# Expert rows weighted as they leave PSUM and added to the residual rows in DRAM by an indirect DMA, in place of a gather in the last stage

## The chip, the cores and the metric

The kernel runs on one core of a Trainium2 chip. The metric is the time of one execution on the device in microseconds (us); three runs of the kernel before took 2931.78, 2933.26 and 2941.8 us, so its median is 2933.26 us. Lower is better.

## What is computed

One layer of a decoder trunk on 2048 tokens of 1024 features, all in float32: RMSNorm, differential attention with a residual add, RMSNorm, a mixture of 32 SwiGLU experts, and a last RMSNorm. The change touches the mixture and what follows it:

```python
g_p   = max(softmax(h @ w_group + b_group))              # 4 groups of 8 experts
top_v, top_i = top_k(e_logits[chosen group], 2)          # two experts per token
top_w = softmax(top_v) * g_p                             # the routing weight
...
# rows sorted by expert, each expert padded to whole blocks of 128 rows
yr = (silu(xb @ w_gate[e]) * (xb @ w_up[e])) @ w_down[e]  # block by block
y  = zeros((T, D)).at[row_tok].add(yr * row_w[:, None])
x  = x + y
out = rms_norm(x, norm_final)
```

So each token gets two expert rows, each times its weight, added to its residual row.

## The kernel before, in words

The program is five stages, each with its own instruction stream per engine, hand-placed semaphores and a barrier between stages: `project` (QKV), `attend`, `mix_and_route`, `run_experts`, `finish`.

**attend** also writes zeros to the spare blocks of the expert output buffer `y_rows`: 32 DMAs of 512 KB from `nil` (L469), spread over the loads of `q_st`.

**mix_and_route** takes the 16 tiles of 128 tokens through a software pipeline five steps deep. Step n on TensorE (PE) is: output projection of tile n-1 (L1164), transpose of tile n (L1172), transpose of tile n-2 (L1179), router matmul of tile n-3 (L1187), rank counts of tile n-4 (L1194). ScalarE (ACT) squares and roots, copies `oT_hi` out of PSUM (L984), and last in its step copies `h2T` (L989). VectorE (DVE) forms x2 and h2, picks experts for tile n-4 (`choose`), places tile n-5 (`place`), and then, as the last thing of its step, writes `oT_lo` of tile n (L1062); the next projection waits for that and for the next x2 (L1039). GpSimd (POOL) scatters each token number into the list `slots` in DRAM (L953). The logits are kept in SBUF (`kept`) for the last stage.

**run_experts** loops over n = 45 blocks of 128 rows (32 experts, each at least one block, read from a table in SBUF). The two splits of every weight, hi on ACT and lo on DVE, make the matmuls three-term. The order of the work is the program order of each engine:

```python
# PE, iteration b
gate_up(b)        # 48 matmuls of 512 columns
turn_x(b + 1)     # waits for the gathered rows of block b+1
down(b)           # 24 matmuls; `down(k)` is of block k-1
turn_h(b)
# POOL, iteration b: waits for turn_x(b-1), loads 128 list entries
# (L1288), waits for them, gathers 128 rows of h2 into xg (L1290)
```

ACT, iteration b: a quarter of the next expert's `gu_hi` split, `act_g`, `x_high(b+1)`, the other three quarters, `take_y(b)` (PSUM to `y_sb`, L1321), `d_hi`, `hT_hi`, then `store_y(b)`: a plain store of 512 KB into `y_rows` (L1325). `take_y` waits for the store before it (semaphore `y_out`). SyncE (SP) loads the 6 MB of weights of the next expert as the splits free the raw buffers (L1270, L782, L783). There are one `xg`, one `listed` and one `y_sb`.

**finish** computes the 16 x 2 routing weights at once, then goes through the tiles in a ring of four: SP loads x2, POOL gathers the two expert rows of each token (L1571, two DMAs of 512 KB a tile), DVE does two multiply-adds (L1627, L1630), ACT square and root, DVE scales, SP stores.

## Time and profile before

| | before |
|---|---|
| median of three runs (lowest, highest) | 2933.26 us (2931.78, 2941.8) |
| profiled execution, span from first to last instruction | 2934.6 us |
| PE / DVE / ACT / POOL busy | 82% / 57% / 43% / 19% |
| `project` | up to about 600 us |
| `attend` | up to about 1564 us |
| `mix_and_route` | up to about 1913 us |
| `run_experts` | up to about 2832 us |
| `finish` | to the end, 103 us |

No own time of the profiled execution stands beside its span in what is shown; the span is 1.3 us above the median of the runs and inside their spread. The stages follow one another with a barrier between them, so each stage's own limit counts in full. The busy shares over the whole span say little, since each stage has another limit: a stage has to be read by its own windows, waits and timeline.

### The profile page before, as it was taken

The numbers are of one execution on the slowest core, as the hardware profiler recorded it, in microseconds if no ns is written. First come the engines' busy times: TensorE is split into PE (matmuls) and PEld (weight loads), VectorE is DVE, ScalarE is ACT, GpSimd is POOL, SyncE is SP. The second block draws the span as 40 slices with busy tenths as digits, with TensorE's granted clock in tenths as the row PEclk, the third lists the DMA queues.
The fourth block names the chain that finished last, engine by engine and source line by source line (L and its number), as shares of the span: only waits on it lengthen the run. The fifth ranks groups of instructions, "written<-read, shape, count | busy, mean of one in ns | idle before, by whom it ended". The sixth has DMA issues, their size and how long they took to land. (4 is left out here: it accounts for less than half of the span.)

```text
span 2934.6 us, 44327 instructions
## 1 busy us (share of the span) xinstructions
PE 2406.7 (82%) x12888; PEld 2029.3 (69%) x12888; DVE 1679.4 (57%) x3485; ACT 1272.2 (43%) x2083; POOL 558.9 (19%) x432
## 2 busy tenths in 40 slices
PE   5999999937687887877885999667899999999930
PEld 4888889926576676766774788555788888787730
DVE  6122122127687776876895566555665665665656
ACT  5111111115475665655774222145554555555533
POOL 0000000004353343443441011110010110111123
PEclk7999999969898998998997999778999999999965
DMA  4333333264515425244122443157768667768758
GB/s 165 115 122 114 122 127 107 90 172 119 147 28 135 108 72 141 68 109 133 59 71 95 176 132 115 51 221 280 297 254 299 251 238 283 291 255 304 277 223 329
DMA packets 263134, 491.03 MB, mean 167 GB/s; under 512 B 24425, under 2 KB 125969, under 8 KB 258898
## 3 DMA queue, kind: packets, MB, share of 16 engines
q1 hardware_dynamic: 218306, 397.31, 39.4%
q0 software_dynamic: 17072, 53.79, 5.6%
q10 hardware_dynamic: 27616, 38.28, 3.9%
q8 instruction: 60, 0.98, 0.1%
q14 instruction: 80, 0.66, 0.1%
HBM read 363.71 MB, written 125.60 MB: 167 GB/s over the span
## 5 line engine op out<-in xcount | busy, mean ns | idle before, releaser
L1372 DVE TENSOR_TENSOR gu_lo<-gu_raw,gu_hi 128x2048 fp32r<-128x2048 f32 x128 | 293.2, 2291 | 162.2 <-ACT gu_hi L1303 118.0
L728 PE MATMUL ps_s<-k_lo,q_st 128*128 128x512 f32 (+3 forms) x640 | 275.7, 431 | 133.7 <-DMA q_st<-qk 68.6
L523 ACT ACTIVATE prob<-prob,shift 128x1024 f32<-128x1024 f32 (+7 forms) x384 | 342.8, 893 | 4.2
L752 PE MATMUL ps_o<-v_hl,aT_hi 128*128 128x256 f32 x1088 | 294.4, 344 | 59.9 <-DVE aT_lo L685 59.0
L608 DVE TENSOR_SCALAR_CACHE_REDUCE prob<-ps_s 128x128 f32<-128x128 f32 (+7 forms) x352 | 276.9, 787 | 114.4 <-PE ps_s L728 111.2
L1303 ACT ACTIVATE gu_hi<-gu_raw 128x2048 fp32r<-128x2048 f32 x128 | 239.0, 1908 | 178.8 <-DMA gu_raw<-in_moe_w_up 101.4
L207 DVE TENSOR_TENSOR stage<-ps,stage 128x512 fp32r<-128x512 f32 (+1 forms) x128 | 71.3, 557 | 427.1 <-ACT stage L162 427.1
L550 ACT ACTIVATE aT_hi<-ps_t 128x512 fp32r<-128x512 f32 (+2 forms) x320 | 168.2, 526 | 306.2 <-PE ps_t L740 223.8
L752 PEld LDWEIGHTS ps_o<-v_hl,aT_hi 128*128 128x128 f32 x1088 | 208.7, 192 | 91.8 <-DVE aT_lo L685 86.8
L162 ACT ACTIVATE stage<-ps 128x512 fp32r<-128x512 f32 (+1 forms) x128 | 62.8, 491 | 474.4 <-PE ps L258 314.8
L508 POOL TENSOR_TENSOR prob<-prob 128x384 f32<-128x384 f32 (+6 forms) x112 | 254.5, 2272 | 9.3
L728 PEld LDWEIGHTS ps_s<-k_lo,q_st 128*128 128x128 f32 x640 | 131.0, 205 | 167.1 <-issue 74.1
L728 PE MATMUL ps_s<-k_hi,q_st 128*128 128x512 f32 (+3 forms) x640 | 245.5, 390 | 0.0
L754 PE MATMUL ps_o<-v_hl,aT_lo 128*128 128x128 f32 x1088 | 244.4, 225 | 0.0
L1464 PE MATMUL ps_g<-gu_hi,xT_lo 128*128 128x512 f32 x720 | 236.6, 410 | 4.3 <-DVE xT_lo L1387 3.6
L1464 PE MATMUL ps_g<-gu_lo,xT_hi 128*128 128x512 f32 x720 | 231.3, 403 | 0.0
L685 DVE TENSOR_TENSOR aT_lo<-ps_t,aT_hi 128x512 fp32r<-128x512 f32 (+2 forms) x320 | 193.1, 605 | 64.8 <-ACT aT_hi L550 64.1
L1464 PE MATMUL ps_g<-gu_hi,xT_hi 128*128 128x512 f32 x720 | 230.0, 400 | 0.0
L506 POOL TENSOR_SCALAR prob<-prob,coef 128x384 f32<-128x384 f32 (+6 forms) x112 | 116.9, 1044 | 581.7 <-DVE coef L646 581.7
L754 PEld LDWEIGHTS ps_o<-v_hl,aT_lo 128*128 128x128 f32 x1088 | 211.7, 195 | 3.6
L1380 DVE TENSOR_TENSOR d_lo<-d_raw,d_hi 128x2048 fp32r<-128x2048 f32 x64 | 146.8, 2294 | 95.7 <-ACT d_hi L1310 81.4
L740 PE MATMUL ps_t<-ident,prob 128*128 128x128 f32 x1088 | 180.7, 283 | 14.5 <-POOL prob L508 9.1
(227 smaller groups left out, 4673.6 us busy)
## 6 DMA issues: line engine op xcount, KB each, us to landing
gu_raw<-in_moe_w_gate SPq DMA_DIRECT2D x128, 512.0 KB, 7.7
gu_raw<-in_moe_w_up SPq DMA_DIRECT2D x128, 512.0 KB, 8.6
d_raw<-in_moe_w_down SPq DMA_DIRECT2D x64, 1024.0 KB, 4.9
qk<-stage SPq DMA_DIRECT2D x64, 512.0 KB, 2.7
y_rows<-y_sb ACTq DMA_DIRECT2D x45, 512.0 KB, 3.4
v<-stage SPq DMA_DIRECT2D x64, 256.0 KB, 2.1
q_st<-qk SPq DMA_DIRECT2D x256, 64.0 KB, 2.4
y_rows<-nil SPq DMA_DIRECT2D x32, 512.0 KB, 3.4
```

Of the source, the lines that this page charges most:

```text
L508: pool.tensor_tensor(p0, p0, p1, ALU.add).then_inc(mixed_p, 1)
L523: nc.scalar.activation(prob[:, r % RING, m, k0:k0 + w], prob[:, r % RING, m, k0:k0 + w], ACT.Exp, bias=shift[:, r % 4, m:m + 1], scale=SCA ...
L550: nc.scalar.activation(aT_hi[:, g % 4, 0:n], ps_t[:, g % 2, 0:n], ACT.Copy).then_inc(t_hi, 1)
L608: ins = nc.vector.tensor_scalar(prob[:, r % RING, m, k0:k0 + far], ps_s[:, c % 2, 0:far], 1.0, None, ALU.mult, ALU.max, accum_out=top[:, r ...
L685: nc.vector.tensor_tensor(aT_lo[:, g % 4, 0:w], ps_t[:, g % 2, 0:w], aT_hi[:, g % 4, 0:w].bitcast(F32), ALU.subtract).then_inc(t_lo, 1)
L728: mm = pe.matmul(ps_s[:, c % 2, j:j + n], q_st[:, x % Q_RING, m, :], k_op[:, half % 2, m, k0 + j:k0 + j + n], start=k_op is k_lo, stop=k_o ...
L740: mm = pe.transpose(ps_t[:, g % 2, (k - k0) * P:(k - k0 + 1) * P], prob[:, r % RING, 0, k * P:(k + 1) * P], ident[:, :])
L752: pe.matmul(ps_o[:, x % 2, 0:2 * P], aT_hi[:, g % 4, t], v_hl[:, half, k, :], start=k == 0, stop=False)
L754: mm = pe.matmul(ps_o[:, x % 2, 0:P], aT_lo[:, g % 4, t], v_hl[:, half, k, 0:P], start=False, stop=k == i)
L1303: nc.scalar.activation(gu_hi[:, j * GC:(j + 1) * GC], gu_raw[:, j], ACT.Copy).then_inc(gu_hi_set, 1)
L1372: nc.vector.tensor_tensor(gu_lo[:, j * GC:(j + 1) * GC], gu_raw[:, j], gu_hi[:, j * GC:(j + 1) * GC].bitcast(F32), ALU.subtract).then_inc( ...
L1464: mm = pe.matmul(ps_g[:, half, :], x[:, cs], w[:, c, half, :], start=c == 0 and k == 0, stop=c == KC - 1 and k == 2)
```

## The change

The routing weights are computed in `mix_and_route`, tile by tile: DVE writes the five exponents' arguments to `x5` in `choose`, ACT does the Exp at the end of its step, DVE waits for that in `place` and writes token number and weight side by side into `tokw`; the scatter to `slots` moves eight bytes a row. In `run_experts` ACT multiplies by the weight as it takes the block from PSUM, ACT's store is gone, and POOL adds the 128 rows into `x2_rows` in DRAM by an indirect DMA with `compute_op=add`. POOL waits for each add to land, then loads the list again into `to_rows` for the next block. Padding rows point to 128 spare rows at the end of `x2_rows` and `h2_rows`. The 32 DMAs of zeros in `attend` become two. `finish` keeps all 16 tiles in SBUF, loads them without a ring and has no gather and no multiply-add. Line numbers in the two `order` blocks marked "of the change" are those of the changed kernel.

```diff
-            spare = scratch["y"].rearrange("(b p) d -> b p d", p=P)[EXPERTS:]
-            PER_PAIR = (BLOCKS_MAX - EXPERTS) // PAIRS
-            EVERY = (NR - Q_RING) // PER_PAIR
+            for rows_ in (scratch["h2"], scratch["x2"]):
+                sp.dma_start(rows_[SEQ:SEQ + P].rearrange("p (k d) -> p k d", k=4),
+                             nil[:, :].unsqueeze(1).to_broadcast([P, 4, D // 4])).then_inc(nil_out, 16)
             def pair(it, more):
...
-                    if (r - Q_RING) % EVERY == 0 and n < PER_PAIR:
-                        sp.dma_start(spare[bass.ds(it * PER_PAIR + n, 1)]
-                                     .rearrange("o p (k d) -> (o p) k d", k=4),
-                                     nil[:, :].unsqueeze(1).to_broadcast([P, 4, D // 4])).then_inc(nil_out, 16)
...
                     for k in range(2):
                         pool.indirect_dma_start(scratch["slots"], bass.IndirectOffsetOnAxis(ap=slot[:, q, k:k + 1], axis=0),
-                                                tok[:, q:q + 1], None).then_inc(scattered, 16)
+                                                tokw[:, q, k, :], None).then_inc(scattered, 16)
...
+                if has(at, 5):
+                    q = 1 - par
+                    act.wait_ge(chosen, (n - 5) * 13 + 13)
+                    nc.scalar.activation(e5[:, q, :], x5[:, q, :], ACT.Exp).then_inc(exped, 1)
...
+            nc.vector.tensor_scalar(empty[:, :, 0], lanes[:, :], P - 1, SEQ, ALU.bitwise_and, ALU.bitwise_or
+                                    ).then_inc(empty_set, 1)
...
+                nc.vector.tensor_scalar(x5[:, q, 0:GROUPS_E], lg[:, 0:GROUPS_E], gm[:, 0:1], None, ALU.subtract)
...
+                nc.vector.tensor_tensor(x5[:, q, 4:5], ev[:, 1:2], ev[:, 0:1], ALU.subtract)
...
+                gate(dve, exped, t + 1, passed)
+                link(nc.vector.tensor_reduce(e_sum[:, :], e5[:, q, 0:GROUPS_E], AX.X, ALU.add))
+                link(nc.vector.scalar_tensor_tensor(out=den[:, :], in0=e5[:, q, 4:5], scalar=1.0, in1=e_sum[:, :],
+                                                    op0=ALU.add, op1=ALU.mult))
+
                 dve.wait_ge(freed, t + (FREED0 - 1))
-                link(nc.vector.tensor_copy(tok[:, q:q + 1], tok_f[:, 0:1]))
+                weight = tokw[:, q, :, 1].bitcast(F32)
+                link(nc.vector.reciprocal(weight[:, 0:1], den[:, :]))
+                link(nc.vector.tensor_tensor(weight[:, 1:2], weight[:, 0:1], e5[:, q, 4:5], ALU.mult))
+                nc.vector.tensor_copy(tokw[:, q, :, 0], tok_f[:, 0:1].to_broadcast([P, 2]))
                 link(nc.vector.tensor_tensor(before[:, :], before[:, :], both[:, q, :], ALU.add))
...
-            pool.iota(iota_i[:, :], pattern=[[1, EXPERTS]], base=0, channel_multiplier=0).then_inc(iota_set, 1)
             n = blocks_of(pool)
-            with pool.Fori(0, n + 1) as b:
...
+            def load_x(b):
...
                 gate(pool, x_turned, b + X_TURNED0, passed)
...
                 gate(pool, listed_in, b * 16 + 16, passed)
                 pool.indirect_dma_start(xg[:, :], None, scratch["h2"],
                                         bass.IndirectOffsetOnAxis(ap=listed[:, 0:1], axis=0)).then_inc(x_in, 16)
+
+            def load_rows(k):
+                at = look(pool, k - 1, COL_LIST, 0, SLOTS - P)
+                pool.dma_start(to_rows[:, :], scratch["slots"][bass.ds(at, P), :]).then_inc(rows_in, 16)
+
+            def add_y(k):
+                gate(pool, y_taken, k + Y_TAKEN0, passed)
+                pool.indirect_dma_start(scratch["x2"], bass.IndirectOffsetOnAxis(ap=to_rows[:, 0:1], axis=0),
+                                        y_sb[:, :], None, compute_op=ALU.add).then_inc(y_out, 16)
+
+            load_x(0)
+            load_x(1)
+            load_rows(1)
+            with pool.Fori(1, n) as b:
+                load_x(b + 1)
+                add_y(b)
+
+                gate(pool, y_out, b * 16, passed)
+                load_rows(b + 1)
+            add_y(n)
+            pool.wait_ge(y_out, n * 16)
+            pool.sem_inc(passed, 1)
...
                 act.wait_ge(d_used, k * DS + D_USED0)
-                act.wait_ge(y_out, k * 16 + (Y_OUT0 - 16))
-                nc.scalar.activation(y_sb[:, :], ps_y[:, :], ACT.Copy).then_inc(y_taken, 1)
-
-            def store_y(k):
-                gate(act, y_taken, k + Y_TAKEN0, passed)
-                act.dma_start(scratch["y"].rearrange("(b p) d -> b p d", p=P)[bass.ds(k - 1, 1)].rearrange("o p d -> (o p) d"),
-                              y_sb[:, :]).then_inc(y_out, 16)
+                act.wait_ge(rows_in, k * 16)
+                nc.scalar.activation(y_sb[:, :], ps_y[:, :], ACT.Copy, scale=to_rows[:, 1:2].bitcast(F32)).then_inc(y_taken, 1)
...
                 nc.scalar.activation(hT_hi[:, :], ps_h[:, :], ACT.Copy).then_inc(h_hi_set, 1)
-                if not first:
-                    store_y(b)
...
+        GROUPS = (0, 1, 2, 2, 3, 3, 3, 3, 4, 4, 4, 4, 5, 5, 5, 5)
+        x_in = [s(f"x_in{k}") for k in range(6)]
...
+            for t in range(TILES):
+                sp.dma_start(acc[:, t, :], x2_rows[t]).then_inc(x_in[GROUPS[t]], 16)
+                if t == 0:
+                    sp.dma_start(g_row[:, :], io["norm_final"].rearrange("(o d) -> o d", o=1).to_broadcast([P, D])).then_inc(g_in, 16)
+            for t in range(TILES):
                 gate(sp, done, t + 1, passed)
-                sp.dma_start(out_rows[bass.ds(t, 1)].rearrange("o p d -> (o p) d"), acc[:, i, :]).then_inc(stored[i], 16)
...
-                    for k in range(2):
-                        pool.indirect_dma_start(y[:, i, k, :], None, scratch["y"],
-                                                bass.IndirectOffsetOnAxis(ap=rows[:, i, k:k + 1], axis=0)).then_inc(y_in[i], 16)
...
+            for t in range(TILES):
+                act.wait_ge(x_in[GROUPS[t]], 16 * GROUPS.count(GROUPS[t]))
+                if t:
+                    act.wait_ge(squared, t)
+                nc.scalar.activation(sq[:, :], acc[:, t, :], ACT.Square, accum_out=ss[:, t:t + 1]).then_inc(squared, 1)
+                act.wait_ge(squared, t + 1)
+                nc.scalar.activation(rt[:, t:t + 1], ss[:, t:t + 1], ACT.Sqrt, bias=eps[:, 0:1], scale=1.0 / D).then_inc(rooted, 1)
...
+            for t in range(TILES):
+                dve.wait_ge(rooted, t + 1)
+                nc.vector.reciprocal(ri[:, t:t + 1], rt[:, t:t + 1]).then_inc(inverted, 1)
+                dve.wait_ge(inverted, t + 1)
+                nc.vector.scalar_tensor_tensor(out=acc[:, t, :], in0=acc[:, t, :], scalar=ri[:, t:t + 1], in1=g_row[:, :],
                                                op0=ALU.mult, op1=ALU.mult).then_inc(done, 1)
...
-            with dve.Fori(0, TILES // RING) as q:
-                for i in range(RING):
-                    dve.wait_ge(x_in[i], q * 16 + 16)
-                    dve.wait_ge(y_in[i], q * 32 + 32)
-                    a = acc[:, i, :]
-                    nc.vector.scalar_tensor_tensor(out=a, in0=y[:, i, 0, :], scalar=w_all[:, 0, bass.ds(q * RING + i, 1)],
-                                                   in1=a, op0=ALU.mult, op1=ALU.add).then_inc(mixed, 1)
-                    dve.wait_ge(mixed, q * RING + (i + 1))
-                    nc.vector.scalar_tensor_tensor(out=a, in0=y[:, i, 1, :], scalar=w_all[:, 1, bass.ds(q * RING + i, 1)],
-                                                   in1=a, op0=ALU.mult, op1=ALU.add).then_inc(added, 1)
...
-            "slots": nc.dram_tensor("slots", (SLOTS, 1), I32).ap(),
-            "y": nc.dram_tensor("y_rows", (BLOCKS_MAX * P, D), F32).ap(),
+            "x2": nc.dram_tensor("x2_rows", (SEQ + P, D), F32).ap(),
+            "h2": nc.dram_tensor("h2_rows", (SEQ + P, D), F32).ap(),
+            "slots": nc.dram_tensor("slots", (SLOTS, 2), I32).ap(),
```

GpSimd in the loop of `run_experts`, of before: one list load and one gather an iteration (`ISA` and `REGISTER_ALU` are waits and register work, `TENSOR_LOAD` reads the block table).

```order
L1256 TENSOR_LOAD block_table
L1256 ISA x2
L36 REGISTER_ALU
L1288 REGISTER_ALU
L1288 DMA listed<-slots 128x1
L36 ISA
L1290 DMA xg<-h_rows,listed 128x1024
L1284 ISA
L1284 COMPARE_AND_BRANCH
```

The same loop of the change, from the list load of `load_x(b + 1)` to the loop's end:

```order
L1289 DMA listed<-slots 128x2
L29 ISA
L1291 DMA xg<-h_rows,listed 128x1024
L1300 DMA x_rows<-y_sb,to_rows 2176x1024
L29 REGISTER_ALU
L1257 ISA
L1257 TENSOR_LOAD block_table
L1257 ISA x2
L1296 ISA
L1296 DMA to_rows<-slots 128x2
L1306 REGISTER_ALU
L1306 COMPARE_AND_BRANCH
```

The add stands behind the gather of the next block, and the next iteration's list load and gather stand behind the add, its landing and the load of `to_rows`.

ScalarE in one step of the loop of `mix_and_route`, of before:

```order
L972 ACTIVATE sq,ss<-x 128x1024
L974 ACTIVATE rt<-ss,eps 128x1
L976 ISA
L978 ACTIVATE sq<-o_t 128x1024
L980 ACTIVATE rth<-ssh,eps 128x8
L981 REGISTER_ALU
L984 ACTIVATE oT_hi<-ps_a,sub_gs 128x1024
L989 ACTIVATE h2T<-ps_c 128x1024
```

The same step of the change:

```order
L966 ACTIVATE sq,ss<-x 128x1024
L968 ACT_TABLE_LOAD
L968 ACTIVATE rt<-ss,eps 128x1
L970 ISA
L972 ACTIVATE sq<-o_t 128x1024
L974 ACTIVATE rth<-ssh,eps 128x8
L975 REGISTER_ALU
L978 ACTIVATE oT_hi<-ps_a,sub_gs 128x1024
L983 ACTIVATE h2T<-ps_c 128x1024
L986 ISA
L987 ACT_TABLE_LOAD
L987 ACTIVATE e<-x 128x5
```

The Exp stands last in the step, with a table load of its own, and the root of the next step needs a second one.

## Rows read from the trace of the kernel before

**Rows 1.** Windows: us, PE, PEld, DVE, ACT, POOL; clock, DMA share, GB/s
```profile
1930.00:2828.00 898.00, 838.72 (x3786) 677.03 (x3784) 546.28 (x329) 476.33 (x367) 94.80 (x90) 0.96 0.72 266
2832.00:2935.00 103.00, 0.00 (x0) 0.00 (x0) 64.03 (x71) 34.90 (x59) 45.59 (x49) 0.50 0.88 331
```

**Rows 2.** Timeline of TensorE, second and last turn of gathered rows: start us, us
```profile
1947.60 1.04 PE L1453 MATMUL ps_x<-ident,xg 128*128 128x128 f32 x8
...
2805.12 1.03 PE L1453 MATMUL ps_x<-ident,xg 128*128 128x128 f32 x8
```

**Rows 3.** Timeline of a block with weights to split and one without
```profile
2308.96 1.03 PE L1453 MATMUL ps_x<-ident,xg 128*128 128x128 f32 x8
...
2316.36 1.01 ACT L1321 ACTIVATE y_sb<-ps_y 128x1024 f32<-128x1024 f32 x1
...
2327.05 1.04 PE L1453 MATMUL ps_x<-ident,xg 128*128 128x128 f32 x8
...
2333.79 1.03 ACT L1321 ACTIVATE y_sb<-ps_y 128x1024 f32<-128x1024 f32 x1 [4.65 <-PE ps_y L1486]
```

**Rows 4.** Waits, 1920 to 2830 us: us in total, times, longest
```profile
POOL listed L1288 <- PE ps_x L1453: 574.2, 45, 20.2
```

**Rows 5.** Timeline of GpSimd in the stretch of rows 3
```profile
2310.72 0.57 POOL L1288 DMA_DIRECT2D listed<-slots  x1 [12.76 <-PE ps_x L1453]
2313.79 2.25 POOL L1290 DMA_INDIRECT xg<-h_rows,listed  x1 [2.50 <-DMA listed<-slots]
2328.82 0.57 POOL L1288 DMA_DIRECT2D listed<-slots  x1 [12.78 <-PE ps_x L1453]
2335.42 0.97 POOL L1290 DMA_INDIRECT xg<-h_rows,listed  x1 [6.03 <-DMA listed<-slots]
```

**Rows 6.** Landing of two gathers (L1290), issued at 2241.4 and 2335.4 us
```profile
DMA to landing us min/median/max: 4.2/4.2/4.2
...
DMA to landing us min/median/max: 7.9/7.9/7.9
```

**Rows 7.** DMA issues of the whole run: KB each, median us to landing
```profile
y_rows<-y_sb ACTq DMA_DIRECT2D x45, 512.0 KB, 3.4
...
xg<-h_rows,listed POOLq DMA_INDIRECT x46, 6.9
```

**Rows 8.** GpSimd: first table look (ns, first start us) and first list load
```profile
L1256 POOLq TENSOR_LOAD <-block_table x47: 289/296/697, 1914.8 to 2765.8; - x47
...
1917.23 0.61 POOL L1288 DMA_DIRECT2D listed<-slots  x1 [3.64 <-issue]
```

**Rows 9.** Timeline of SyncE: the first load of the next weights
```profile
2326.49 0.37 SPq L782 DMA_DIRECT2D gu_raw<-in_moe_w_gate  x1
```

**Rows 10.** Timeline of TensorE after an idle stretch
```profile
2820.69 1.22 PE L1486 MATMUL ps_y<-d_hi,hT_lo 128*128 128x512 f32 x2 [8.50 <-DVE hT_lo L1411]
...
2824.48 0.63 PE L1486 MATMUL ps_y<-d_hi,hT_hi 128*128 128x512 f32 x2
```

**Rows 11.** Timeline of one tile of the routing stage
```profile
1680.16 1.28 DVE L1062 SCALAR_TENSOR_TENSOR oT_lo<-ps_a,sub_gs,oT_hi 128x1024 fp32r<-128x1024 f32 x1 [0.79 <-ACT oT_hi L984]
...
1681.66 1.02 ACT L989 ACTIVATE h2T<-ps_c 128x1024 f32<-128x1024 f32 x1 [1.53 <-PE ps_d L1187]
...
1682.72 5.50 PE L1164 MATMUL ps_b<-wo_hi,oT_lo 128*128 128x512 f32 x16 [0.72 <-DVE x L1039]
```

**Rows 12.** Timeline: a table load and an Exp on ScalarE in the last stage
```profile
2832.36 1.28 ACT L1578 ACT_TABLE_LOAD   x1 [3.31 <-PEq L1210]
...
2833.81 0.20 ACT L1579 ACTIVATE e_v<-e_v 128x16 f32<-128x16 f32 x1
```

**Rows 13.** Waits, 600 to 1700 us
```profile
PE ps_s L728 <- DMA q_st<-qk: 68.6, 6, 13.1
```

**Rows 14.** Timeline of GpSimd where the weights come late: two successive list loads
```profile
2008.76 0.57 POOL L1288 DMA_DIRECT2D listed<-slots  x1 [18.44 <-PE ps_x L1453]
...
2036.38 0.57 POOL L1288 DMA_DIRECT2D listed<-slots  x1 [19.46 <-PE ps_x L1453]
```

More of the change, by code:

```diff
@@ L843, in mix_and_route @@
         ps_e = ctx.enter_context(nc.psum_tensor("ps_e", [P, 512], F32))
-        ident, start, kept, e_all, rank_all = (keep[k] for k in ("ident", "start", "kept", "e_all", "rank_all"))
+        ident, start = keep["ident"], sb("start", [P, EXPERTS])
         s = lambda name: sem("c_" + name)
@@ L931, in _ @@
         def _(pool):
-            pool.memset(zeros[:, :], 0).then_inc(made, 1)
+            pool.memset(empty[:, :, :], 0).then_inc(made, 1)
             pool.memset(ones[:, :], 1.0).then_inc(made, 1)
@@ L963, in _ @@
             act.wait_ge(gain_set, 1)
-            act.wait_ge(made, 9)
+            act.wait_ge(made, 10)
             def step(n, par, at):
@@ L1066, in choose @@
             def choose(t, q):
-                link = chain(chosen, t * 14)
+                link = chain(chosen, t * 13)
                 dve.wait_ge(routed, t + (1 + ROUTED0))
@@ L1152, in _ @@
             pe.sem_inc(h2T_set, H2T0)
-            pe.wait_ge(made, 10)
+            pe.wait_ge(made, 11)
             def step(n, par, at):
@@ L1235, in run_experts @@
         ps_y = ctx.enter_context(nc.psum_tensor("ps_y", [P, D], F32))
-        ident, start, e_all, rank_all, dest = (keep[k] for k in ("ident", "start", "e_all", "rank_all", "dest"))
+        ident = keep["ident"]
         s = lambda name: sem("d_" + name)
@@ L1519, in finish @@
-        w_all = sb("w_all", [P, 2, TILES])
         eps = sb("eps55", [P, 1])
-        ss, rt, ri = sb("ss5", [P, RING]), sb("rt5", [P, RING]), sb("ri5", [P, RING])
-        kept, dest = keep["kept"], keep["dest"]
+        ss, rt, ri = sb("ss5", [P, TILES]), sb("rt5", [P, TILES]), sb("ri5", [P, TILES])
         s = lambda name: sem("e_" + name)
-        g_in, x_in, y_in = s("g_in"), [s(f"x_in{i}") for i in range(RING)], [s(f"y_in{i}") for i in range(RING)]
-        rows_set, weigh, exped, mixed, eps_set = s("rows"), s("weigh"), s("exped"), s("mixed"), s("eps")
@@ L1543, in _ @@
-            for i in range(RING):
-                load(i, i)
-            def store(t, i):
-                gate(sp, done, t + 1, passed)
-                sp.dma_start(out_rows[bass.ds(t, 1)].rearrange("o p d -> (o p) d"), acc[:, i, :]).then_inc(stored[i], 16)
-            with sp.Fori(0, TILES // RING - 1) as q:
-                for i in range(RING):
-                    store(q * RING + i, i)
-                    if i >= 1:
-                        load(q * RING + (RING + i - 1), i - 1)
-                load(q * RING + (2 * RING - 1), RING - 1)
@@ L1556, in _ @@
-            for i in range(RING):
-                store(TILES - RING + i, i)
-            for i in range(RING):
-                sp.wait_ge(stored[i], 16 * TILES // RING + STORED0)
+            for t in range(TILES):
[3 more added lines that the diff above has]
+            for t in range(TILES):
+                gate(sp, done, t + 1, passed)
+                sp.dma_start(out_rows[t], acc[:, t, :]).then_inc(stored, 16)
@@ L1563, in _ @@
             pool.memset(eps[:, :], 1e-6).then_inc(eps_set, 1)
-            with pool.Fori(0, TILES // RING) as q:
-                for i in range(RING):
-                    gate(pool, added, q * RING + (i + 1), passed)
-                    pool.tensor_copy(rows[:, i, :], dest[:, bass.ds(q * (2 * RING) + 2 * i, 2)]).then_inc(rows_set, 1)
-                    gate(pool, rows_set, q * RING + (i + 1), passed)
-                    for k in range(2):
-                        pool.indirect_dma_start(y[:, i, k, :], None, scratch["y"],
-                                                bass.IndirectOffsetOnAxis(ap=rows[:, i, k:k + 1], axis=0)).then_inc(y_in[i], 16)
```

123 lines of the change are left out of this document (22 added, 101 removed).

## The prediction

> **What bounds the kernel now.** The stages are separated by barriers, so I read each by itself. The windows come first: in the expert stage TensorE is busy 839 of 898 us at a granted clock of 0.96, the DMA engines 72% [rows 1]. That stage is bound by TensorE. The last stage is bound by its DMAs: 103 us at a DMA share of 0.88 and 331 GB/s, with no engine above 64 us [rows 1]. The timeline then gives the length of a block. From the second turn of gathered rows to the last, 44 blocks later, pass 2805.12 - 1947.60 = 857.5 us, 19.5 a block [rows 2]; two blocks at full speed are 2327.05 - 2308.96 = 18.1 us apart [rows 3]. The waits say why GpSimd never held TensorE up: it waits 574 us in 45 waits, 12.8 us each, for the turn that frees `xg` [rows 4]. Its list load and gather run ahead of the need, during one whole block.
>
> **The experts: a chain closes.** This part decides. TensorE's order is `gate_up(b)`, `turn_x(b+1)`, `down(b)`. In the change GpSimd's list load and gather for `turn_x(b+2)` stand behind `add_y(b)`, behind the wait for its landing and behind the load of `to_rows`. `add_y(b)` waits for `take_y(b)`, that for `down(b)`, and that stands on TensorE behind `turn_x(b+1)`. So from one turn to the next runs one chain, and nothing in it overlaps; only `gate_up` lies beside it. Its parts:
>
> 1. Turn to the end of `take_y`: with weights to split 2316.36 + 1.01 - 2308.96 = 8.4 us, without 2333.79 + 1.03 - 2327.05 = 7.8 us [rows 3]. ACT's multiply by a weight in place of a plain copy is costed at nothing: it is the same instruction with another scale. The store that leaves ACT's queue stood behind other work: nothing.
> 2. Semaphore to GpSimd's DMA: the turn ends at 2309.99, the list load starts at 2310.72: 0.7 us [rows 3, 5].
> 3. The add to its landing: no row has an adding DMA. The nearest is the indirect gather of the same 128 rows of 4 KB, median 6.9 us; the plain store of the same tile lands in 3.4 us, and gather and store one after the other are 7.9 + 3.4 = 11.3 us [rows 6, 7]. I take 6.9: same queue, same rows, DRAM read as well. The ends are 3.4 and 11.3; it can't be less than nothing, since GpSimd waits for it.
> 4. From landing to the next list load: a look into the table, the load of `to_rows`, another look. The first two looks and one issue took 1917.23 - 1914.8 = 2.4 us [rows 8]; with 0.57 for the second DMA and 0.6 before it, 3.6 us.
> 5. List load to gather: 2313.79 - 2310.72 = 3.1 us where no weights were just issued, 2335.42 - 2328.82 = 6.6 us behind them [rows 5].
> 6. Gather to landing: 4.2 us alone, 7.9 us behind weights [rows 6].
>
> The weights of the next expert are issued once DVE has split the last ones, 2326.49 - 2308.96 = 17.5 us behind the turn [rows 3, 9]; the list load comes 8.4 + 0.7 + 6.9 + 3.6 = 19.6 us behind it, right after them. So where there are weights the dear values hold: 8.4 + 0.7 + 6.9 + 3.6 + 6.6 + 7.9 = 34.1 us. Where there are none: 7.8 + 0.7 + 6.9 + 3.6 + 3.1 + 4.2 = 26.3 us. `gate_up` of the next block starts behind `down` and ends before the gather has landed. Of 44 periods 31 have weights (32 experts, one loaded ahead): 31 x 34.1 + 13 x 26.3 = 1399 us, against 857.5: **+542 us**. TensorE will idle some 16 of 34 us. After 8.5 idle us a pair of matmuls took 1.22 us where 0.63 is usual [rows 10], which lasts some 3 us, so 1.5 us are lost; with weights this hides behind ACT's splits, which end as late as `down`, without it lengthens the chain: 13 x 1.5 = **+20 us**.
>
> A page of the Trainium skill prices the transfers lower: "DMA: Bandwidth & Descriptors", in its section on the anatomy of a DMA on the gpsimd path, gives about 2.0 us plus bytes over 436 GB/s, which is an estimate of 3.2 us for 512 KB and 2.0 for the list. By that the period would be 8.4 + 0.7 + 3.2 + 3.6 + 2.0 + 3.2 = 21.1 us, and the stage only +71 us. The trace does not agree: a gather alone needs 4.2 us and one behind weights 7.9 [rows 6].
>
> **The routing stage.** Today `oT_lo` starts at 1680.16 and the projection that waits for it and for x2 at 1682.72 [rows 11]; VectorE has a little slack before it. In the change `place` stands in front of `oT_lo` and waits for the Exp, which ACT does at the end of its step, behind `h2T`: 1681.66 + 1.02 = 1682.68 [rows 11], then a table load of 1.28 and the Exp, 0.2 [rows 12]: 1684.2. Then six small operations, costed at the 0.2 of the Exp beside them: `oT_lo` starts at 1685.4, 5.2 us later, and TensorE has nothing left to do. Steps 5 to 15 pay it in full, 57 us; of the five steps that drain the pipeline the first pays 5.2 and the others some 1.2 each for the longer `place`: 10 us. Colder restarts of TensorE, as above: 8. Together **+75 us**, between 40 (if half hides) and 107 (6.7 us in all 16 steps). The second table load, before the root, lies beside the projection. The larger list to clear and the wider scatter stand on GpSimd, which first scatters over 100 us into the stage: nothing; without that cover they would cost a microsecond or two.
>
> **The last stage.** It moved 103 us x 331 GB/s = 34 MB. Without the 32 gathers 17.3 MB are left; at the same rate 52 us. **-51 us.** ACT's squares and roots lie beside: with them ACT was busy only 34.9 of 103 us [rows 1]. If latency at both ends tells more, -40; at the best rate, -58.
>
> **The rest.** In the attention stage 30 stores of zeros go. TensorE waits 68.6 us for `q_st` in six waits [rows 13]; a store of 512 KB ahead of it can cost about a microsecond each: **-5 us**, at most -68. The last add lands later than the last store did: **+4 us**.
>
> **Sum.** 2934.6 + 542 + 20 + 75 - 51 - 5 + 4 = 3520 us. This is made against the span of the profiled execution, 1.3 us above the median of the runs, which changes nothing here.
>
> **Rivals.**
> - *Hidden anyway (faster).* The add, its list and their waits cost GpSimd 6.9 + 3.6 + 0.7 = 11.2 us a block, and it idles 12.8 [rows 4]; so the expert stage stays at 19.5 a block, the last stage saves 51, and the Exp is hidden too: 2934.6 - 51 - 5 + 10 = 2889 us. It decides if the chain is shorter than 19.5 us. Against it: the idle time of GpSimd lies before the turn, and the add can't start before `down`. 3 in 100, and 1 in 100 that it comes out level.
> - *Bare transfers.* The DMA load falls with the longer period, and all transfers cost their quiet price: 8.4 + 0.7 + 3.4 + 3.6 + 3.1 + 4.2 = 23.4 us with weights, 22.8 without: 1022 us, +164, in all about 3140. 4 in 100. The rule of the page above points this way.
> - *The weights bind instead.* As before, but where weights come late the blocks were already 2036.38 - 2008.76 = 27.6 us apart [rows 14], since loads, splits and `take_y` make a loop of their own. 31 x 27.6 + 13 x 22.8 = 1152 us, +295: about 3270. 12 in 100.
> - *A dear add.* It reads its destination as well as its source, and takes 11.3 us: + 4.4 x 44 = 194, about 3715. 10 in 100. "Collectives: The Full Stack" of the Trainium skill, on why ReduceScatter is half of AllGather, says that an add emits two reads for one write; no row here shows it.
>
> **How the numbers follow.** 70 in 100 for the forecast, whose own range is 3400 to 3650. The range of 3250 to 3680 takes in the third rival and the near part of the fourth and leaves out the rest. A measurement can tell about 0.5% here, 15 us. Faster 0.03, within 0.01, slower 0.96: only the first rival is not slower.
>
> **What would show it.** In the changed profile turns of gathered rows (the PE rows of `ps_x`) stand some 34 and 26 us apart; TensorE waits there for the DMA of `xg`, over 450 us in total; GpSimd waits for `y_sb` and for the add's landing. The adding DMA lands in about 7 us. In the routing stage VectorE waits for ACT's Exp and a tile takes some 5 us more than before. The last stage takes some 52 us. I am wrong if TensorE still turns rows every 20 us, or if the list load overtakes the add.

## The result, and the profile after

The change makes the kernel slower by a fifth: median 3525.35 us (3522.68 to 3527.32, four runs) against 2934.98 us (2931.78 to 2941.8, four runs), a ratio of 1.2004 with a 95% interval of 1.1986 to 1.2021. The profiled execution took 3522.68 us, its span is 3520.5 us. The prediction was 3520, with a range of 3250 to 3680.

The windows of the changed kernel, from the second turn of gathered rows to the last, from there to the last stage, and the last stage (us; busy us of PE, PEld, DVE, ACT, POOL; granted clock, DMA share, GB/s):

```profile
2030.50:3435.10 1404.60, 883.92 (x3673) 711.44 (x3671) 534.61 (x316) 470.84 (x359) 205.70 (x174) 0.82 0.52 166
3435.10:3475.00 39.90, 16.08 (x60) 12.70 (x60) 6.50 (x4) 7.34 (x6) 3.85 (x3) 0.71 0.17 26
3475.00:3520.00 45.00, 0.00 (x0) 0.00 (x0) 22.09 (x32) 23.07 (x49) 0.10 (x1) 0.50 0.97 385
```

They answer to [rows 1]. The 44 periods that took 857.5 us now take 1404.6. No engine and no queue is full in them: TensorE is busy 63% of the time, where it was over 90%, and the DMA share fell to 0.52. Of the stages, the last alone became shorter. The waits between 1930 and 3500 us (us in total, times, longest) show who waits for whom:

```profile
POOL x_rows L1300 <- ACT y_sb L1344: 681.5, 45, 17.7
...
PE ps_x L1443 <- DMA xg<-h_rows,listed: 543.8, 44, 24.9
...
POOL to_rows L1296 <- issue: 313.9, 44, 10.8
...
POOL xg L1291 <- DMA listed<-slots: 184.6, 45, 6.3
```

TensorE, which never waited for `xg`, waits 543.8 us for it in 44 waits. GpSimd's wait moved from the turn [rows 4] to `y_sb`, and 313.9 us stand in front of the load of `to_rows`, put down to "issue"; that is the wait for the add to land, which the code puts there and the profile doesn't name. One whole period in the timeline (TensorE, ScalarE, GpSimd; start us, us):

```profile
2595.98 1.97 PE L1443 MATMUL ps_x<-ident,xg 128*128 128x128 f32 x8 [12.42 <-DMA xg<-h_rows,listed]
...
2604.31 1.10 ACT L1344 ACTIVATE y_sb<-ps_y,to_rows 128x1024 f32<-128x1024 f32 x1
...
2606.30 3.38 POOL L1300 DMA_INDIRECT x_rows<-y_sb,to_rows  x1 [13.65 <-ACT y_sb L1344]
2615.79 0.59 POOL L1296 DMA_DIRECT2D to_rows<-slots  x1 [6.10 <-issue]
2617.46 0.55 POOL L1289 DMA_DIRECT2D listed<-slots  x1 [1.08 <-issue]
2623.85 1.02 POOL L1291 DMA_INDIRECT xg<-h_rows,listed  x1 [5.84 <-DMA listed<-slots]
...
2630.99 1.97 PE L1443 MATMUL ps_x<-ident,xg 128*128 128x128 f32 x8 [15.30 <-DMA xg<-h_rows,listed]
```

This is the chain of the prediction, link by link: 9.4 us from the turn to the end of `take_y`, 0.9 to the add, 9.5 until it has landed and `to_rows` is asked for, 1.7 to the list load, 6.4 to the gather, 7.1 to the turn: 35.0 us.

In the routing stage VectorE and ScalarE do this in front of one projection:

```profile
1757.26 1.02 ACT L983 ACTIVATE h2T<-ps_c 128x1024 f32<-128x1024 f32 x1 [1.53 <-PE ps_d L1192]
1758.30 1.28 ACT L987 ACT_TABLE_LOAD   x1
1759.60 0.21 ACT L987 ACTIVATE e<-x 128x5 f32<-128x5 f32 x1
...
1759.93 0.16 DVE L1104 TENSOR_REDUCE e_sum<-e 128x1 f32<-128x4 f32 x1 [7.89 <-ACT e L987]
...
1761.09 1.28 DVE L1062 SCALAR_TENSOR_TENSOR oT_lo<-ps_a,sub_gs,oT_hi 128x1024 fp32r<-128x1024 f32 x1
1762.28 1.21 DVE L1039 TENSOR_TENSOR x<-ps_b,x 128x1024 f32<-128x1024 f32 x1
```

VectorE idles 7.89 us for the Exp. `oT_lo` starts 3.8 us behind the start of `h2T`; in [rows 11] it started 1.5 us before it. That is 5.3 us later.

Where the 585.9 us between the two spans went:

| part | forecast | measured | from |
|---|---|---|---|
| start and attention | -5 | +4.8 | first projection of the routing stage 1597.0, now 1601.8 |
| routing | +75 | +78.1 | second turn 1947.6, now 2030.5, less 4.8 |
| 44 periods | +542 + 20 | +547.1 | 857.5, now 1404.6 |
| last turn to the last stage | +4 | +12.9 | 2805.1 to 2832.3, now 3435.1 to 3475.2 |
| last stage | -51 | -57.0 | 102.3, now 45.3 |

### The profile page after: what moved, and what is told of

Same layout as the page of the kernel before. It is cut to its first block and busy times, and to the rows that moved or that the text cites. A ratio compares the mean times of both kernels' runs of the same rounds, so it can differ in the third digit from the quotient of the medians.

```text
span 3520.5 us, 44205 instructions
## 1 busy us (share of the span) xinstructions
PE 2502.9 (71%) x12888; PEld 2103.1 (60%) x12888; DVE 1642.6 (47%) x3473; ACT 1309.5 (37%) x2120; POOL 631.3 (18%) x474
## 5 line engine op out<-in xcount | busy, mean ns | idle before, releaser
L1443 PE MATMUL ps_x<-ident,xg 128*128 128x128 f32 x368 | 88.7, 421 | 543.8 <-DMA xg<-h_rows,listed 543.8
L1443 PEld LDWEIGHTS ps_x<-ident,xg 128*128 128x128 f32 x368 | 70.9, 220 | 563.0 <-DMA xg<-h_rows,listed 562.7
L716 PE MATMUL ps_s<-k_lo,q_st 128*128 128x512 f32 (+3 forms) x640 | 274.3, 429 | 138.5 <-DMA q_st<-qk 74.2
L1399 DVE TENSOR_TENSOR xT_lo<-ps_x,xT_hi 128x1024 fp32r<-128x1024 f32 x46 | 56.3, 1224 | 492.3 <-ACT xT_hi L1337 492.3
L1337 ACT ACTIVATE xT_hi<-ps_x 128x1024 fp32r<-128x1024 f32 x46 | 47.2, 1027 | 515.2 <-PE ps_x L1443 515.2
L1300 POOL DMA_INDIRECT x_rows<-y_sb,to_rows x45 | 112.8, 2507 | 681.5 <-ACT y_sb L1344 681.5
## 6 DMA issues: line engine op xcount, KB each, us to landing
k_lo<-qk SPq DMA_DIRECT2D x28, 512.0 KB, 13.3
```

Of the source, the lines that this page charges most:

```text
L716: mm = pe.matmul(ps_s[:, c % 2, j:j + n], q_st[:, x % Q_RING, m, :], k_op[:, half % 2, m, k0 + j:k0 + j + n], start=k_op is k_lo, stop=k_o ...
L1300: pool.indirect_dma_start(scratch["x2"], bass.IndirectOffsetOnAxis(ap=to_rows[:, 0:1], axis=0), y_sb[:, :], None, compute_op=ALU.add).then ...
L1443: mm = pe.transpose(ps_x[:, c * P:(c + 1) * P], xg[:, c * P:(c + 1) * P], ident[:, :])
```

## The experiments

The chain was the theory. Its rivals after the result: the adding DMA is dear wherever it stands; the loop of the weights (their loads and splits) binds; the Exp costs by its operations, not by its place. Landings are counted from the start of the issue. Each run's times are the medians, each ratio is against the kernel before on the same chip.

**1. The gather ahead of the add**

```diff
             load_rows(1)
+            load_x(2)
             with pool.Fori(1, n) as b:
-                load_x(b + 1)
+                load_x(b + 2)
                 add_y(b)
...
             add_y(n)
+            pool.wait_ge(x_in, n * 16 + 32)
```

> Only GpSimd's order changes: list load and gather of block b+2 stand ahead of the add of block b-1, and no longer behind it, its landing and the load of to_rows. Everything else of the changed kernel, the adds too, stays. Theory (the chain from turn to turn closes through the add): a turn frees xg, list load and gather run beside down and gate_up as in the kernel before, the turns come back to about 19.7 us apart, 44 x 19.7 = 867 us in place of the 1406 us measured from the second turn to the last, so about 3525 - 539 = 2986 us (2960 to 3010), and TensorE's wait for xg is under 60 us. Rival (the adding DMA itself is too dear: it takes 1.6 to 3.4 us of GpSimd, lands in 7.8 and holds up the transfers beside it): turns stay over 27 us apart and the time over 3300.

Measured: 3010.68 us, ratio 1.0249 (1.0225 to 1.0272): 515 us came back by moving one call. The periods sum to 897.7 us. The chain is the cause of nearly all of the loss, and the dear-add rival falls. TensorE's wait for `xg` fell to 42.2 us. But the time is 0.7 us above the range that I gave: 40 us are missing in the periods, 20.4 us each and not 19.5. GpSimd's timeline in this kernel says where a part of them is:

```profile
2436.47 1.01 POOL L1291 DMA_INDIRECT xg<-h_rows,listed  x1 [5.36 <-DMA listed<-slots]
2437.78 3.37 POOL L1300 DMA_INDIRECT x_rows<-y_sb,to_rows  x1 [0.30 <-issue]
2449.90 0.59 POOL L1296 DMA_DIRECT2D to_rows<-slots  x1 [8.75 <-issue]
2451.58 0.55 POOL L1289 DMA_DIRECT2D listed<-slots  x1 [1.09 <-issue]
2454.68 1.02 POOL L1291 DMA_INDIRECT xg<-h_rows,listed  x1 [2.55 <-DMA listed<-slots]
```

GpSimd waits for nobody there but its own DMAs: gather to gather are 18.2 us, with 12.1 from the start of the add to the load of `to_rows`, which waits for its landing. It has become as long as a block. Without the list's wait 20 us of the missing time come back (experiment 6 against 5), and experiment 10 finds the rest.

**2. The add without the sum**

```diff
-                                        y_sb[:, :], None, compute_op=ALU.add).then_inc(y_out, 16)
+                                        y_sb[:, :], None).then_inc(y_out, 16)
```

> The indirect DMA writes its rows without adding; the sum with the residual and of the two experts is left out. Same chain, same rows and bytes to write. Theory (the chain counts the landing in full, and reading the destination is part of the 7.8 us): the landing falls to about 5, GpSimd's issue to 1.0, so 44 x 3 = 130 us off, about 3395 (3330 to 3450). Rival (the add as such is free, 7.8 us is what any scatter of 128 rows takes here): within 15 us of 3525. Second rival (only the issue is dearer): 44 x 1.5 = 66 off, and the landing counted from the issue's end stays.

Measured: 3438.45 us, ratio 1.1697 (1.1678 to 1.1717), 87 us off; the periods sum to 1323.0 us, 1.9 us less each. The landings of this line, in the changed kernel and here (here up to 3380 us, without the last one):

```profile
DMA to landing us min/median/max: 6.1/7.8/12.6
```

```profile
DMA to landing us min/median/max: 3.4/4.7/9.8
```

The median landing falls by 3.1 us, and 1.9 of it reach the period. The rest meets the same traffic one link on: the gather behind it lands in 5.9 us (median) and no longer in 4.4. The theory holds in kind; its 3 us a period were too many. The first rival (the add as such is free) falls. So does the second (only the issue is dearer): the issue falls from 2.5 to 1.8 us on average, and the landing counted from its end still falls from 5.7 to 3.6. The packets of GpSimd's queue (packets, MB, share of the 16 engines' span), in the changed kernel and here:

```profile
q0 software_dynamic: 20448, 60.96, 7.5%
```

```profile
q0 software_dynamic: 20448, 60.96, 5.1%
```

Same packets and same bytes. With the sum they keep the DMA engines 0.075 x 3520.5 - 0.051 x 3437.1 = 89 us longer, 2.0 us an add. What an add costs the DMA engines can't be read from the bytes in these traces.

**3. The list ahead, the gather behind the add**

```diff
+            def load_list(b):
                 at = look(pool, b, COL_LIST, 0, SLOTS - P)
+                gate(pool, x_in, b * 16, passed)
+                pool.dma_start(listed[:, :], scratch["slots"][bass.ds(at, P), :]).then_inc(listed_in, 16)
...
             with pool.Fori(1, n) as b:
                 load_x(b + 1)
+                load_list(b + 2)
                 add_y(b)
```

> The list for the next gather is loaded as soon as the gather before has landed, ahead of the add; the gather itself stays behind the add. Theory (chain terms add up one by one): the list's 6.4 us behind weights and 3.1 us without leave the chain, 31 x 6.4 + 13 x 3.1 = 239 us off, about 3286 (3240 to 3330). Rival (the list only waits out a burst of weight traffic that the gather would then meet): the gather's landing grows by what the list saves, and less than 120 us come off. Second rival (the loop of the weights binds at 27.6 us): the periods with weights stop at 27.6 and TensorE's waits turn from xg to the weights' splits.

Measured: 3361.11 us, ratio 1.1437 (1.1417 to 1.1456), 164 us off: between the theory's 239 and the rival's 120. The periods are 3.7 us shorter. The list's landing left the chain, and the gather's landing grew from a median of 4.4 us to 7.2 (line of the gather, in the changed kernel and here):

```profile
DMA to landing us min/median/max: 4.1/4.4/7.9
```

```profile
DMA to landing us min/median/max: 4.2/7.2/7.9
```

So these links of the chain do not simply add up: one of them waits out traffic that the next would meet. TensorE still waits for `xg` 380.8 us, so the loop of the weights doesn't bind even at 28 us a period.

**4. The Exp at the head of ScalarE's step**

```diff
             def step(n, par, at):
+                if has(at, 5):
+                    q = 1 - par
+                    act.wait_ge(chosen, (n - 5) * 13 + 13)
+                    nc.scalar.activation(e5[:, q, :], x5[:, q, :], ACT.Exp).then_inc(exped, 1)
                 if has(at, 2):
...
                     nc.scalar.activation(h2T[:, :], ps_c[:, :], ACT.Copy).then_inc(h2T_set, 1)
-                if has(at, 5):
-                    q = 1 - par
-                    act.wait_ge(chosen, (n - 5) * 13 + 13)
-                    nc.scalar.activation(e5[:, q, :], x5[:, q, :], ACT.Exp).then_inc(exped, 1)
```

> Only the routing stage changes: ACT does the Exp of tile n-5 at the head of its step, ahead of Square and Sqrt, and not behind the copy of h2T. Theory (VectorE waits for that Exp just before it writes oT_lo, on which the next projection hangs): the wait goes, the tile period falls from 23.7 us towards 17.3 plus at most 1.3 for a table load ahead of the root, so 16 tiles x 4 to 6 = 64 to 96 us off, of the 78 us that the stage grew by; about 3455 (3435 to 3475). Rival (the added small operations on VectorE and the two table loads a step are the cost, wherever the Exp stands): less than 25 us off.

Measured: 3449.29 us, ratio 1.1734 (1.1714 to 1.1753), 76 us off. In the trace the second turn moves from 2030.5 to 1960.0, 70.6 us, and the periods stay at 1404.3 in sum. Three successive tiles start their projections so:

```profile
1689.44 3.88 PE L1169 MATMUL ps_b<-wo_hi,oT_lo 128*128 128x512 f32 x16 [1.07 <-DVE x L1039]
1706.59 6.76 PE L1169 MATMUL ps_b<-wo_hi,oT_lo 128*128 128x512 f32 x16 [1.62 <-DVE x L1039]
1725.26 3.88 PE L1169 MATMUL ps_b<-wo_hi,oT_lo 128*128 128x512 f32 x16 [0.72 <-DVE x L1039]
```

They are 17.9 us apart on average. Two in the changed kernel are 23.7 us apart:

```profile
1739.82 6.61 PE L1169 MATMUL ps_b<-wo_hi,oT_lo 128*128 128x512 f32 x16 [1.35 <-DVE x L1039]
...
1763.55 2.93 PE L1169 MATMUL ps_b<-wo_hi,oT_lo 128*128 128x512 f32 x6 [1.19 <-DVE x L1039]
```

The place was the cost. Both table loads and the small operations are still there and cost some 8 us in the whole stage.

**5. Both orders together**

The edits of experiments 1 and 4, of which the two calls that move:

```diff
-                load_x(b + 1)
+                load_x(b + 2)
                 add_y(b)
...
             def step(n, par, at):
+                if has(at, 5):
+                    q = 1 - par
+                    act.wait_ge(chosen, (n - 5) * 13 + 13)
+                    nc.scalar.activation(e5[:, q, :], x5[:, q, :], ACT.Exp).then_inc(exped, 1)
```

> The edits of e1_gather_first and e4_exp_first together. Theory (two separate causes, which add up): the turns of e1 (897.7 us from the second to the last) and the routing stage of e4 (70.6 us shorter than in the changed kernel), so 3010.7 - 70.6 = about 2940 us (2930 to 2950), level with the kernel before. Rival (the two share a cover): over 2960.

Measured: 2942.55 us, ratio 1.0022 (1.0012 to 1.0031), within the theory's range. The two causes are separate and add up.

**6. The lists ahead as well**

```diff
             with pool.Fori(1, n) as b:
-                load_x(b + 1)
+                load_x(b + 2)
                 add_y(b)
+                load_list(b + 3)
```

> As e5_first_and_first, and each list is loaded as soon as the gather before it has landed, beside the landing of the add. Theory (in e1 GpSimd's own row of waits, list 4 + gather 1.3 + add 3 + landing 6 to 10 + next loads 1.7 us, had become as long as a block, and made it 20.4 us in place of 19.5): without the list's wait it has 4 us to spare, the turns take the 857.5 us of the kernel before or up to 8 more, and the time is 2940 - 35 = about 2905 us (2890 to 2920), faster than before. Rival (the adds' traffic holds up the weights): the turns stay above 885 us and the time above 2925.

Measured: 2923.16 us, ratio 0.9955 (0.9942 to 0.9969): the one version with the full sum that is faster than both kernels, 12 us faster than the kernel before. It is 3 us above the range that I gave. GpSimd has slack again (it waits 305.6 us for `y_sb`), and 36 of the 44 periods are 18.1 us, as in the kernel before. The periods sum to 881.7 us, though, 24 more than before. They lie in the seven long ones: 28.9 to 32.3 us, where the kernel before had 25.5 to 29.6. So the theory holds for the short periods, and something like the rival for the long ones; experiment 10 tests that.

**7. The zeros put back**

```diff
+                    n = (r - Q_RING) // EVERY
+                    if (r - Q_RING) % EVERY == 0 and n < PER_PAIR:
+                        sp.dma_start(spare[bass.ds(it * PER_PAIR + n, 1)]
+                                     .rearrange("o p (k d) -> (o p) k d", k=4),
+                                     nil[:, :].unsqueeze(1).to_broadcast([P, 4, D // 4])).then_inc(nil_out, 16)
```

> The changed kernel with the 32 stores of zeros of the attention stage put back, into rows that nothing reads. In the trace of before the first projection of the routing stage starts at 1597.0, in those of the changed kernel and four versions of it at 1599.4 to 1601.8, and TensorE waits 74 to 76 us for q_st in place of 68.6. Theory (the stores cost nothing, and by spacing the loads of q_st they even helped by 3 us): q_st back to 67 to 71 us, first projection near 1597. Rival (those microseconds lie in something else): q_st stays at 74 to 76. Second rival (my term of -5): q_st over 78.

Measured: 3520.51 us, ratio 1.1984 (1.1966 to 1.2003), whose interval overlaps that of the changed kernel. First projection at 1602.9, wait for `q_st`:

```profile
PE ps_s L725 <- DMA q_st<-qk: 72.8, 6, 13.4
```

None of the three theories, as far as one trace tells: with the stores back the wait is 72.8 us, without them 74.2 in the changed kernel, with the kernel before at 68.6. The stores of zeros cost and bring nothing that shows.

**8. Thin splits on VectorE**

```diff
-                    nc.vector.tensor_tensor(gu_lo[:, j * GC:(j + 1) * GC], gu_raw[:, j],
-                                            gu_hi[:, j * GC:(j + 1) * GC].bitcast(F32), ALU.subtract).then_inc(gu_split, 1)
+                    nc.vector.tensor_tensor(gu_lo[:, j * GC:(j + 1) * GC, :, 0:16], gu_raw[:, j, :, :, 0:16],
+                                            gu_hi[:, j * GC:(j + 1) * GC, :, 0:16].bitcast(F32), ALU.subtract).then_inc(gu_split, 1)
```

and the same for `d_lo`; both are set to zero once ahead of the loop.

> The changed kernel with VectorE's splits of the weights cut to 16 columns of each row; the low parts of the weights are left out otherwise. In the trace of the changed kernel GpSimd's issue of the add takes 1.64 us in 14 of 45, and up to 3.4 in the others, longer by as much as a 128x2048 split of VectorE runs beside it. Theory (GpSimd can't write the descriptors while VectorE runs such an operation): all 45 issues take 1.6 to 1.7 us, and about 40 us come off the chain for it, more if the weights land earlier; the landing behind the issue stays at 5.9 to 10. Rival (the DMA traffic stretches the issue): the issues still spread from 1.6 to 3.4.

Measured: 3503.25 us in one run. The line of the add (instructions, ns min/median/max), first in the changed kernel between 2020 and 3270 us, then here:

```profile
L1300 POOL DMA_INDIRECT x_rows<-y_sb,to_rows x38: 1639/2458/3420, 2054.9 to 3250.1; - x38
```

```profile
L1300 POOL DMA_INDIRECT x_rows<-y_sb,to_rows x43: 1635/1647/1679, 2051.0 to 3399.6; - x43
...
DMA to landing us min/median/max: 7.5/8.0/9.4
```

On the issue the theory's numbers are right: all 45 take 1.62 to 1.68 us. Its reason is another matter (last section). On the time it isn't right: the periods sum to 1392.4 us, 12 less and not 40. From the start of the add to the load of `to_rows` it is 9.67 us on average, against 9.70. What the issue saves, the landing takes: in the changed kernel (between 2050 and 2700 us) it had been

```profile
DMA to landing us min/median/max: 6.1/7.9/11.7
```

so its minimum rose from 6.1 to 7.5 us. The splits free the raw buffers earlier here: behind the add at 2477.0 us the next load of `d_raw` is issued after 1.4 us and the add lands in 7.9, behind the one at 2482.7 us of the changed kernel it is issued after 3.5 us and the add lands in 6.3. So more weights may be under way; that part wasn't tested.

**9. List and gather between the add's issue and its landing**

```diff
             load_rows(1)
+            load_x(2)
             with pool.Fori(1, n) as b:
-                load_x(b + 1)
                 add_y(b)
+                load_x(b + 2)
```

> The changed kernel, but GpSimd puts list load and gather between the issue of the add and the wait for its landing: they stand behind add and down still, no longer behind landing and to_rows. Theory (the wait on the landing and the to_rows load are terms of the chain, GpSimd's queue of DMAs is none): 7.8 + 1.7 us leave each period, so 32 - 9 = 23 us a turn and about 3525 - 400 = 3125 us (3060 to 3200). Rival (the DMAs of GpSimd's queue run one after the other, so list and gather wait for the add's bytes anyway): only to_rows' 1.7 us and little more goes, 3400 or above.

Measured: 3297.77 us, ratio 1.1236 (1.1217 to 1.1255): 225 us off, between both. The periods sum to 1180.6 us, 5.1 less each. GpSimd's timeline:

```profile
2441.37 3.36 POOL L1300 DMA_INDIRECT x_rows<-y_sb,to_rows  x1 [13.35 <-ACT y_sb L1346]
2444.14 1.21 POOL L1289 DMA_DIRECT2D listed<-slots  x1
2453.93 1.00 POOL L1291 DMA_INDIRECT xg<-h_rows,listed  x1 [8.58 <-DMA listed<-slots]
2455.14 0.57 POOL L1296 DMA_DIRECT2D to_rows<-slots  x1 [0.22 <-issue]
```

The list, 1 KB, needs 9.8 us to the gather behind an add, and as soon as the gather is issued the add has landed too (0.22 us of waiting). This is so all through the stage: in 42 of 44 blocks the list lands 0.1 to 0.4 us behind the add, in two 1.6 and 1.9 us. So a small load behind the add in the same queue came home with it, not before. Add with its landing, `to_rows` and list were 9.7 + 1.7 + 4.6 = 16 us of each period in the changed kernel (means over all periods); from the add to the gather it is now 9.5. The two waits no longer follow one another, but the longer of them stays: 6.5 us are saved there, of which 5.1 reach the period; a part of the rest is the gather, which lands later (6.3 us on average, against 5.5). The rival had the mechanism right and the size wrong: it forgot that the list's own wait lies beside the landing then.

**10. Experiment 6 without the sum**

The edit of experiment 2 in the kernel of experiment 6:

```diff
-                                        y_sb[:, :], None, compute_op=ALU.add).then_inc(y_out, 16)
+                                        y_sb[:, :], None).then_inc(y_out, 16)
```

> e6_lists_ahead_too with a plain scatter in place of the add; the sum is left out. In e6 39 of the 45 periods are 14.9 to 18.1 us, as before, and 6 or 7 where each block has new weights take 28.9 to 32.3 us, where the kernel before has 25.5 to 29.6. Theory (the adds read the rows that they add to, 512 KB more a block, and that holds up the weights where they bind): the long periods fall by 1 to 3 us each, the time by 8 to 20 us to about 2910. Rival (the long periods come from something that both have, GpSimd's issues or the order of the transfers): within 5 us of 2923.

Measured: 2897.59 us, ratio 0.9869 (0.9853 to 0.9886); by the ratios 25 us less than experiment 6, more than the theory's 20. The periods (window from the second turn to the last, experiment 6 and this one) sum to 881.7 and 856.8:

```profile
1954.60:2836.30 881.70, 810.36 (x3674) 655.04 (x3672) 529.77 (x314) 469.39 (x358) 222.44 (x173) 0.95 0.80 263
```

```profile
1956.70:2813.50 856.80, 811.96 (x3673) 655.58 (x3672) 530.50 (x315) 469.72 (x358) 181.47 (x174) 0.97 0.75 271
```

The busy time of TensorE is the same to 2 us; all of the difference is waiting in the seven long periods, where the blocks wait for their weights: ScalarE's waits for `gu_raw` fall from 144.0 us to 99.7, and the kernel before had 101.4. There the sum costs 3.6 us a period (the seven add up to 214.8 us with it and to 189.6 without). In the 37 others it costs nothing. Without the sum the periods take what they take in the kernel before (857.5), so the 24 us that experiment 6 lacked are the sum's.

**11. The kernel before, a second trace**

> The kernel before once more, for a second trace. In its first trace the first projection of the routing stage starts at 1597.0 us and TensorE waits 68.6 us for q_st; in nine traces of changed kernels, one of them with the zeros put back, it is 1599.1 to 1602.9 and 72.8 to 76.8. If the difference belongs to the kernels, this trace shows 1597 and 68 to 69 again; if it is scatter between executions, it can lie anywhere up to 1602 and 76. Turns from the second to the last: 857.5 again, within 3.

Measured: first projection at 1594.7, `q_st` 69.1 us, the periods 860.8 us in sum. The periods are 0.3 us over what I allowed. The 5 us more of `q_st` in the attention stage thus seem to belong to the changed kernels, all eleven traces of them (1597.6 to 1602.9; 72.8 to 76.8), also where the zeros are back. What they all have otherwise in common, other sizes and places of the buffers in DRAM for one, was not tried. The cause stays open.

## Why the prediction was right, step by step

The mechanism was right, and so were the sizes of its large terms. That the sum came within 1 us of the span is luck: the periods came out 15 us and the last stage 6 us under the forecast, and routing 3, the end of the expert stage 9 and the start with attention 10 us over it.

**The chain.** Right, and shown by experiment 1. The parts, as means over the 29 periods of more than 31 us and the 14 of less (the first of the 44 is 14.9 us, its gather had run ahead):

| part | forecast long / short | measured long / short |
|---|---|---|
| 1 turn to end of `take_y` | 8.4 / 7.8 | 9.9 / 9.9 |
| 2 to the add | 0.7 / 0.7 | 0.9 / 0.9 |
| 3, 4 add to its landing, `to_rows`, to the list load | 10.5 / 10.5 | 12.4 / 9.4 |
| 5 list to gather | 6.6 / 3.1 | 4.7 / 4.5 |
| 6 gather to turn | 7.9 / 4.2 | 5.9 / 4.6 |
| period | 34.1 / 26.3 | 33.8 / 29.3 |
| number | 31 / 13 | 29 / 14 |

The sum came out 15 us under the forecast of 1399 + 20 because errors of both signs met. Part 1 was too small: after each idle stretch the turn takes 1.97 us and not 1.03, and the first matmuls 1.20, which I had priced at 1.5 us in 13 periods and which cost about that in all of them; the table of part 1 shows it also where weights are split. TensorE's granted clock over all periods is 0.82 of full speed against 0.97; in the turn behind an idle stretch it is 0.50, the lower of its two levels (1.2 and 2.4 GHz), and that turn takes the 1.97 us. Parts 5 and 6 were too large in the long periods. I had put the list behind the weights that were issued 2 us ahead of it; but the gathers of the changed kernel land in 4.4 us (median), near the 4.2 of a quiet one, and the list takes 4.7. So the weights were mostly through by then; that a longer period leaves their queue more room is my reading, not tested. In the short periods the list is dearer than in the quiet: 4.5 and not 3.1.

**The add.** Forecast 6.9 us with bounds of 3.4 and 11.3, measured 7.8 (6.1 to 12.6; the last two, with no weights under way, 6.4 and 6.2): the gather of the same rows was the right neighbour, and 0.9 us too cheap. No add came near the lower bound, and seven passed the upper one. The dear add (11.3) was wrong as a mean, which is 8.2. It was right that an add costs more than a scatter, 7.8 against 4.7. "Collectives: The Full Stack" of the Trainium skill, on why ReduceScatter is half of AllGather, has two source reads for its add; the traces count no further bytes for this one, but 2.0 us more of the DMA engines an add (experiment 2).

**Bare transfers.** The other rule of the Trainium skill, 2.0 us plus bytes over 436 GB/s in "DMA: Bandwidth & Descriptors", section on the anatomy of one DMA, would make an estimate of 3.2 us of a gather; the fastest of the changed kernel took 4.1. Its period of 21.1 us was never near: after the first, none of the changed kernel's is under 28.3.

**The weights bind.** Wrong as a bound at 27.6 us. In experiment 9 periods fall to 23.3 us and TensorE still waits for `xg`.

**Routing.** Forecast 75, measured 78.1; place of the Exp shown by experiment 4.

**The last stage.** Forecast -51 at the old rate of 331 GB/s, measured -57.0, at 385: the stage, now without gathers, moves its bytes faster. The end of the expert stage cost 12.9 and not 4: from the issue of the last add (3461.89) to the next stage (3475.2) pass 13.3 us, where from the issue of the last store 3.0 passed. Only 6.2 of them are the add's landing. No engine works in the 7.1 us behind it, and what they are stays open; in experiments 1, 5, 6, 9 and 10 the whole stretch took 9.9 to 10.2.

**Attention.** Forecast -5, measured +4.8: wrong in sign, too small to matter, and open. The price of about a microsecond that the forecast gave a store of zeros stands in no row: in experiment 7 the stores cost nothing that shows.

## What to carry to other kernels

Before a transfer is added to an engine's in-order queue, write down what stands behind it there and whether that is what the bound engine waits for next: 547 us came from one call on the wrong side of another, and 515 of the whole loss went with moving it. An engine that is busy 18% of the span can still set the pace when its waits stand in the wrong order. With the order right the adding DMA is a fair trade here, 12 us faster than the gather at the end, and its price lies only where transfers already bind.

## What the runs showed of the hardware

- GpSimd's issue of an indirect DMA is stretched while VectorE runs a subtraction of two 128x2048 tiles in SBUF. In the changed kernel 15 of the 45 adds took 1.62 to 1.65 us to issue (they overlap with a subtraction for at most 0.7 us), the 30 others, with 0.6 to 2.9 us of overlap, 2.15 to 3.42; with thin splits all 45 took 1.62 to 1.68. The stretch is shorter than the overlap, by 0.1 to 1.1 us. The plain loads that GpSimd issues from the same queue are not stretched: 13 list loads of the changed kernel lie wholly beside such a subtraction and take 0.55 to 0.56 us like the rest, and in experiment 2 so do 31 loads of `to_rows` at 0.58. So it isn't the writing of descriptors as such that stands still. The Trainium skill, "SBUF — State Buffer", section "SBUF: two separate sides", says that a VectorE operation with two inputs in SBUF takes the shared ports only against a GpSimd operation that reads SBUF. The trace agrees if the indirect DMA is one for reading its row numbers there, which is my reading; the same section's lock-out from writing descriptors is said of a perf-mode copy. What the stretch costs the period no run shows alone: in experiment 8 it went, the landings rose, and 12 us of 1404.6 came off.
- An add of 128 rows of 4 KB takes 2.0 us more of all 16 DMA engines than a scatter of the same rows (experiment 2), with the same bytes in the record. With no other transfers beside it, it lands in 6.2 us where the scatter takes 3.3 (the last one of the changed kernel and of experiment 2).
- A 1 KB load behind such an add, in the same queue, lands with it: in experiment 9 it takes 5.4 us (median) and up to 10.2, in the changed kernel, not behind an add, 3.8 and up to 6.0.
